# Seven stage boundaries of a two-block transformer kernel, done by token parts, with the double norm's down projection ended tile by tile

## The reference, cut to what matters

```python
def first_block(x, ...):          # two layers
    for i in range(2):
        mix = sconv_ssd_mixer(...) if i % 2 == 0 else fox_mixer(...)
        x = layer_norm(ALPHA * x + mix, ln_mix_g[i], ln_mix_b[i])
        x = layer_norm(ALPHA * x + conv_ffn(x, ...), ln_ffn_g[i], ln_ffn_b[i])
    return x

def second_block(x, c, ...):      # two layers, mod = silu(c) @ ada_w[i] + ada_b[i]
    for i in range(2):
        h = modulate(rmsnorm(x, norm1_g[i]), sh1, sc1)
        y = gqa_attention(h, ...) if i % 2 == 0 else chunked_gmlp(h, ...)
        x = x + g1 * y
        h = modulate(rmsnorm(x, norm2_g[i]), sh2, sc2)
        x = x + g2 * sq_relu_mlp(h, mlp_w_in[i], mlp_w_out[i])
    return x
```

## Time and profile before

| | |
|---|---|
| median of three runs | 2811.45 us (2811.03 to 2812.35) |
| the profiled execution | 2811.43 us, of which 2809.5 us are the profile's span |
| PE busy | 2783.7 us, 99% of the span |
| DVE, ACT, POOL busy | 1303.3, 1081.2 and 1140.6 us |
| granted clock of PE, mean | 0.998 |

### The profile page before, as it was taken

One profiled execution on the slowest core, in us unless ns is written; L12 is line 12 of the kernel. 1 busy time (PEld: TensorE's weight loads), 2 busy tenths in 40 slices (PEclk: granted clock), 3 DMA queues, 4 the chain that ended last, 5 costly groups with the idle time before them and its releaser, 6 DMA issues.

```text
span 2809.5 us, 37915 instructions
## 1 busy us (share of the span) xinstructions
PE 2783.7 (99%) x13890; PEld 2287.7 (81%) x13890; DVE 1303.3 (46%) x1516; ACT 1081.2 (38%) x1574; POOL 1140.6 (41%) x472
## 2 busy tenths in 40 slices
...
GB/s 160 90 69 74 90 103 267 239 140 88 99 88 95 9 76 232 244 169 102 97 73 45 2 74 106 97 105 98 86 135 94 90 78 103 90 92 96 104 98 75
DMA packets 319812, 299.95 MB, mean 107 GB/s; under 512 B 16268, under 2 KB 251224, under 8 KB 319576
## 3 DMA queue, kind: packets, MB, share of 16 engines
...
...
## 4 chain that ended last, share of the span: by engine, by line
PE 46%; issue 36%; POOL 16%; DVE 1%; ACT 0%; POOLq 0%; DVEq 0%; ACTq 0%
POOL wlo L558 16%; PE ps L2034 8%; PE ps L2035 8%; PE ps L2036 8%; PE ps L1892 6%; PE ps L1894 6%; PE ps L1893 6%; PE ps L2319 1%; PE ps L2255 1%; PE ps L2284 1%; PE ps L2394 1%; PE ps L2065 0%; PE ps L2067 0%; PE ps L2066 0%; PE ps L1897 0%
## 5 line engine op out<-in xcount | busy, mean ns | idle before, releaser
L558 POOL TENSOR_TENSOR wlo<-raw,whi 128x1024 fp32r<-128x1024 f32 x444 | 1115.3, 2515 | 1630.6 <-ACT whi L616 1630.3
L1892 PE MATMUL ps<-xhi,whi 128*128 128x512 f32 x1824 | 718.0, 394 | 0.3
L1894 PE MATMUL ps<-xhi,wlo 128*128 128x512 f32 x1824 | 710.3, 389 | 0.0
L1893 PE MATMUL ps<-xlo,whi 128*128 128x512 f32 x1824 | 709.9, 389 | 0.0
L616 ACT ACTIVATE whi<-raw 128x1024 fp32r<-128x1024 f32 x444 | 466.3, 1052 | 288.9 <-PE ps L2036 167.8
L2034 PE MATMUL ps<-whi,ahi 128*128 128x512 f32 x1184 | 461.4, 390 | 0.7 <-DVE alo L1396 0.7
L2036 PE MATMUL ps<-whi,alo 128*128 128x512 f32 x1184 | 460.7, 389 | 0.0
L2035 PE MATMUL ps<-wlo,ahi 128*128 128x512 f32 x1184 | 460.6, 389 | 0.0
L1892 PEld LDWEIGHTS ps<-xhi,whi 128*128 128x128 f32 x1824 | 342.5, 188 | 73.1 <-issue 3.2
L1894 PEld LDWEIGHTS ps<-xhi,wlo 128*128 128x128 f32 x1824 | 342.3, 188 | 71.7
L1893 PEld LDWEIGHTS ps<-xlo,whi 128*128 128x128 f32 x1824 | 342.6, 188 | 71.0 <-issue 1.4
...
## 6 DMA issues: line engine op xcount, KB each, us to landing
...
```

What stands on the lines that cost most here:

```text
L558: pool.tensor_tensor(wlo[:, j], raw[:, j], whi[:, j].bitcast(F32), ALU.subtract).then_inc(w_lo, 1)
L1892: pe.matmul(out, lh, rh, start=start, stop=False)
L1893: pe.matmul(out, lh, rl, start=False, stop=False)
L1894: return pe.matmul(out, ll, rh, start=False, stop=stop)
```

## The change

All seven boundaries run by parts of the tokens. At the six that are called PARTED a part is two tiles: when tiles 0 and 1 are normalized they are transposed and brought to `xhi` and `xlo` as 128 x 256 blocks, and the next projection's first units (in `pe_f` stages units 0, 1 and then 2, with 256 moving columns) take them while tiles 2 and 3 are still on their way. k = 4 to 7 stay whole, their 16 transposes now stand together, and the transposes of constants are gone. At q = 4 the last four units of dn1 run tile by tile (`pe_t_deep`), the parts are tiles (0, 1), 2 and 3, and qkv's first two units follow by these groups. Number 2 of the weight splits moves in ACT's order at q = 1, 2, 3 behind the first part and std(2), at q = 5 and 7 it stands just ahead of the first part.

```diff
-NRM_ORDER = ((0, 0), (1, 0), (0, 1), (2, 0), (3, 0), (1, 1), (2, 1), (3, 1))
-KEEP_BUSY = (0, 18, 0, 16)
+PARTED = (1, 2, 3, 5, 6, 7)
+PART = (slice(0, 256), slice(256, 512))
+DOUBLE_TILES = ((0, 1), (2,), (3,))
+DOUBLE_PART = (slice(0, 256), slice(256, 384), slice(384, 512))
+DEEP = "dn1"
...
+    def act_xt_part(act, q, scale, bias, h, cols=PART):
+        c = cols[h]
+        for k in range(4):
+            act.wait_ge(xt_tp, XT0[q] + 4 * h + k + 1)
             if k >= 2:
-                act.wait_ge(xt_lo, KD * q + k - 1)
+                act.wait_ge(xt_lo, XT0[q] + 4 * h + k - 1)
+            act.activation(xf[:, k % 2, c], ps[:, k, c], ACT.Identity, scale=scale(k), bias=bias(k)).then_inc(xt_ev, 1)
...
         act_next_whi(act, name, 1)
         act_sqrt_table(act, r)
-        for t in range(NT):
-            act_ln_std(act, r, t)
-            if t == 1:
-                act_next_whi(act, name, 2)
+        act_ln_std(act, r, 0)
+        act_ln_std(act, r, 1)
+        act_xt_part(act, r + 1, scale, bias, 0)
+        act_ln_std(act, r, 2)
+        act_next_whi(act, name, 2)
+        act_ln_std(act, r, 3)
         load_gb(act, gb, g_ap, b_ap)
+        act_xt_part(act, r + 1, scale, bias, 1)
+        act_xt(act, r + 1, scale, bias, 4)
...
+    def dve_xt_part(dve, q, h, cols=PART):
+        c = cols[h]
+        for k in range(4):
+            dve.wait_ge(xt_ev, EV0[q] + 4 * h + k + 1)
+            dve.tensor_copy(xhi[:, k, c], xf[:, k % 2, c]).then_inc(xt_hi, 1)
+            dve.wait_ge(xt_hi, XT0[q] + 4 * h + k + 1)
+            dve.tensor_tensor(xlo[:, k, c], xf[:, k % 2, c], xhi[:, k, c].bitcast(F32), ALU.subtract).then_inc(xt_lo, 1)
...
+        for h in range(2):
+            dve_ln_moments(dve, r, name, h and 3)
+            if not h:
+                dve_ln_moments(dve, r, name, 1)
+            for t in (2 * h, 2 * h + 1):
+                dve_ln_inverse(dve, r, t)
+                norm(t, 0)
+            if not h:
+                dve_ln_moments(dve, r, name, 2)
+            dve_xt_part(dve, r + 1, h)
         for t in range(NT):
-            dve_ln_moments(dve, r, name, t)
-            if t:
-                dve_ln_inverse(dve, r, t - 1)
-                norm(t - 1, 0)
-            if t == 2:
-                norm(0, 1)
-        dve_ln_inverse(dve, r, 3)
-        norm(3, 0)
-        for t in range(1, NT):
             norm(t, 1)
+        dve_xt(dve, r + 1, resid=r, k0=4)
...
         dve.wait_ge(gb_in, 32 * (r + 1))
         for t in range(NT):
+            if t == 3:
+                dve_xt_part(dve, 4, 0, DOUBLE_PART)
             dve_ln_moments(dve, r, name, t)
             if t:
-                affine(t - 1)
-            if t >= 2:
-                inverse(t - 2)
-        affine(3)
-        inverse(2)
+                inverse(t - 1)
+            affine(t)
+        dve_xt_part(dve, 4, 1, DOUBLE_PART)
         inverse(3)
+        dve_xt_part(dve, 4, 2, DOUBLE_PART)
...
-            for k in range(KD):
-                pe.wait_ge(xt_lo, KD * q + k + 1)
+            for h in range(2):
+                for k in range(4):
+                    pe.wait_ge(xt_lo, XT0[q] + 4 * h + k + 1)
+                    for e in range(2):
+                        if not h and k == 0:
+                            pe.wait_ge(w_lo, S + e + 1)
+                            pe.wait_ge(res_add, 8 * q - 3 + e)
+                        product(e, k, PART[h])
+                if h:
+                    for k in range(4, KD):
+                        pe_xt_late(pe, q, k)
+                for k in range(4):
+                    if not h and k == 0:
+                        pe.wait_ge(w_lo, S + 3)
+                        pe.wait_ge(res_add, 8 * q - 1)
+                    if not h and k == 3:
+                        pe_xt_part(pe, q, 1)
+                    product(2, k, PART[h])
+            for k in range(4, KD):
+                pe.wait_ge(xt_lo, XT0[q] + 4 + k + 1)
                 for e in range(3):
...
-            if q and q != 4 and t == 2 and i:
-                pe_xt_tile(pe, q, 0)
-        if q:
-            for t in range(0 if q == 4 else 1, NT):
-                pe_xt_tile(pe, q, t)
-                if t == 1:
-                    pe.wait_ge(res_add, 8 * q - 3)
-                pe_busy(pe, KEEP_BUSY[t])
+            if q in PARTED and (t, i) == ((2, 1) if q < 4 else (3, 0)):
+                pe_xt_part(pe, q, 0)
+
+    def pe_t_deep(pe, name, q):
+        H, S, A = PAIRS[name], U0[name], A0[name]
+        for t in range(NT):
+            for m in range(2 * H - 4, 2 * H):
...
+                if t == NT - 1:
+                    ins.then_inc(unit_done, 1)
+                    if m == 2 * H - 3:
+                        pe_xt_part(pe, q, 0)
```

More of the change, by code:

```diff
@@ L618, in build_in, with a_parts @@
     AHEAD = 3
+    def a_parts(name, m):
+        first = 2 * PAIRS[name] - 3
+        if name == DEEP and first <= m < first + 2:
+            return ahi2[:, m - first], alo2[:, m - first]
+        return ahi[:, m % 2], alo[:, m % 2]
     def bank_f(j):
@@ L1407, in dve_jit @@
         after_h0()
-        run(dve, H - 2, lambda e, j: step(H + 2, 2, e, j))
+        if name != DEEP:
+            run(dve, H - 2, lambda e, j: step(H + 2, 2, e, j))
+        else:
+            run(dve, H - 5, lambda e, j: step(H + 2, 2, e, j))
+            for m in range(2 * H - 3, 2 * H):
+                hi, lo = a_parts(name, m)
+                dve.wait_ge(a_hi, A + m + 1)
+                dve.tensor_tensor(lo, src[:, 2 * (m - H):2 * (m - H) + 2], hi.bitcast(F32), ALU.subtract).then_inc(a_lo, 1)
     def wait_tile(eng, r, name, t):
@@ L1653, in dve_rms_tail, with tile @@
         dve.tensor_scalar(mv[:, :, 1], sumsq[:, :, 0], 1.0 / D, EPS, ALU.mult, ALU.add).then_inc(half_sq, 1)
-        for t in range(NT):
+        def tile(t):
             wait_tile(dve, 4 + s, name, t)
             dve_gated_tile(dve, s, 1, t)
-            if t:
-                inverse(t - 1)
-                norm(t - 1, 0)
-            if t == 2:
-                norm(0, 1)
-        inverse(3)
-        norm(3, 0)
-        for t in range(1, NT):
+        tile(0)
+        tile(1)
+        for t in range(2):
+            inverse(t)
+            norm(t, 0)
+        tile(2)
+        dve_xt_part(dve, 5 + s, 0)
+        tile(3)
+        for t in range(2, 4):
+            inverse(t)
+            norm(t, 0)
+        dve_xt_part(dve, 5 + s, 1)
+        for t in range(NT):
             norm(t, 1)
+        dve_xt(dve, 5 + s, k0=4)
     def dve_last_tail(dve, s, name):
@@ L1963, in unit @@
             ins.then_inc(unit_done, 1)
-        for s, v in first:
-            pe.wait_ge(s, v)
         if q == 0:
@@ L2019, in pe_f, with pe_t_unit @@
                     unit(i * RING + j, j)
-    def pe_t_unit(pe, start, e, j, bank0, lh, ll, first, blocks=None):
+    def pe_t_unit(pe, start, e, j, bank0, lh, ll, first, blocks=None, tiles=range(NT), done=True, mid=None):
         slot = (start + j) % RING
@@ L2027, in pe_t_unit @@
         for k in range(2):
+            if mid and k:
+                mid()
             if blocks is not None:
                 pe.wait_ge(xt_lo, blocks + k + 1)
-            for t in range(NT):
+            for t in tiles:
                 out = ps[:, bank0 + t]
@@ L2092, in pe_t_jit @@
             unit(h * H, 0, 0, True)
-            if h:
+            if h and name == DEEP:
+                run(pe, H - 5, lambda e, j: unit(H + 1, e, j, False))
+                pe_t_deep(pe, name, q)
+            elif h:
                 run(pe, H - 3, lambda e, j: unit(H + 1, e, j, False))
```

231 lines of the change are left out of this document (145 added, 86 removed).

## The result

The changed kernel takes 2818.77 us (median of 10 runs, 2817.13 to 2820.53), the kernel before 2811.44 us (10 runs, 2810.41 to 2812.35): 1.0025 times as long, 95% interval 1.0017 to 1.0034. So it is slower, by 7.3 us. Its profiled execution has a span of 2815.8 us, 6.3 us more than that of before; the rest of the 7.3 is told of further down. Its times also scatter more, over 3.4 us against 1.9.

A forecast was written before the change was run, and what follows sets the result against it. PE, busy 99% of the span, was taken as the bound. Terms +5.1 (q=1,2,3), +1.3 (q=5,7), -1.3 (q=6), -5.4 (q=4) and +2.45 (clock) gave +2.1 on 2811.43: 2813.5 us, range 2799 to 2819.

The forecast's parts named there:

- (a) to (f): At q = 1, 2, 3: PE's successive waits through a LayerNorm boundary, the last 2.35 us for block 7, summing to 5.75.
- the first wait: At q = 5 and 7: POOL's split holds the first cast by 1.8 us, PE waits 2.2 before its first product.
- the hold: POOL's weight split and DVE exclude each other, so a DVE cast or subtract beside a split ends about 2 us later.
- the price of q = 1: Waits worked out with q = 1's clock and applied to q = 1, 2, 3 alike: +1.7 us each.
- +1.7 each, +5.1 for three: At q = 1, 2, 3: waits of 5.75 us plus 0.47 for half blocks, less 4.55 saved, at each boundary.
- The wait of 5.0 us at q = 4: PE waits 5.0 us for unit 2's late weight split; the clock then falls to half, costing 2.45 us.
- The rival that the clock falls at other places: Clock also falls in waits at q = 1, 2, 3, 5, 7: +12.3 us, 2825.8; chance 0.15 with dearer 256-column matmuls.
- The holds don't fall on the critical blocks: At q = 1 to 5 and 7 DVE comes before POOL's split, blocks finish in time: -13.5, 2800.1 us; chance 0.20.
- The slower rival: Clock falls at five more boundaries, each costing 2.45 us more: 2825.8 us; chance 0.15 with dearer 256-column matmuls.
- waits of 0.1: At q = 1, 2, 3 from k = 4: DVE takes 2.2 us a block, PE 2.04, giving waits of 0.2, 0.1, 0.1.

The follow-up runs named there:

- Run 3: Changed kernel with part 0 of q = 5 and 7 written by ACT into PSUM and read there by DVE: 2817.43 us.
- run 1: Changed kernel with `wf_lo` made directly behind block 7's `xlo`, ahead of the last three residual operations of q = 2: 2813.27 us.
- run 6: Changed kernel with the residual's four shifts at q = 1, 2, 3 adding only one column of 1024: 2805.99 us.
- run 7: Changed kernel with 34 transposes of constants on PE ahead of its wait for `wf_lo` at q = 2: 2818.08 us.
- run 4: Changed kernel with ACT's split of unit 2 at q = 4 moved just ahead of `xf` block 4: 2814.58 us.
- run 2: Changed kernel with all eight residual operations at q = 1, 2, 3 behind block 7: 2825.78 us.
- run 5: Changed kernel with block 7's cast and subtract ahead of one residual shift, shift(1), at q = 1, 2, 3: 2818.92 us.
- run 8: Kernel before the change without its 34 transposes of constants at each of the seven boundaries: 2826.44 us against 2811.28.
- run 10: Changed kernel with q = 1, 2, 3 as before, the PSUM edit at q = 5 and 7 and q = 4's earlier split: 2801.75 us.
- run 9: Changed kernel with earlier `wf_lo`, block 7 ahead of shift(1), part 0 through PSUM at q = 5 and 7, and q = 4's earlier split: 2803.64 us.

## Why the prediction was right or wrong

**Right: five boundaries and their mechanism.** The waits (a) to (f) at q = 1 and 3 are in the trace in that order, 0.55, 0.34, 0.44, 0.80, short ones, and 1.90 (as the profile counts idle time; from pace to pace the last is 2.06), against forecasts of 0.6, 0.7, 0.6, 1.0, 0.5 and 2.35. The steps came out at 1.6 and 1.9 for a forecast 1.7. The prediction's own list adds up to 5.65 and not 5.75, which changes nothing here. At q = 5 and 7 the first wait is 2.0 for 2.2, at q = 6 the step is -1.4 for -1.3. 256-column matmuls start every 0.12 us, as taken. Run 3 shows the hold to be what it was called, by its operand.

**The time: inside the range by luck.** 2818.77 lies 0.23 us below the range's upper end of 2819, and four of the ten executions lie above it. The forecast of 2813.5 stood for a change that can't be told from none; the measured +7.3 can. Of the 5.3 us between forecast and median, q = 2 has 4.8, the other six boundaries together -0.8, the stretch before the first of them 0.3, and 1.0 is the median above the profiled execution.

**Wrong: one term, q = 2.** The prediction gave all three LayerNorm boundaries the price of q = 1. Of the residual's end it said that nobody waits for it. At q = 2 one reader stands behind it: `wf_lo`, which PE needs right after unit 3, 24 matmuls later. And the chain there begins otherwise. The change also moved the load of `wf_raw` behind the last `xf` (785.60; it was 769.12), which the prediction doesn't name. ACT waited 1.8 us for it, and POOL's split of unit 3 started at 789.20, behind the start of block 7's subtract (788.91), so block 7 wasn't held at all. That the late load set this order is argued; no run puts the load back. The holds fell on the three last residual operations and on `wf_lo`: 4.4 us of wait and 2.5 us of clock in place of the 2.35 us for block 7. The step was +6.5 for a forecast +1.7, and run 1 took 6.8 us away with one moved instruction. So the step that failed is the term "+1.7 each, +5.1 for three": at q = 2 it priced at nothing what stands behind the residual.

**Right in kind, off in size: the clock.** The wait of 5.0 us at q = 4 was 4.75 and did cost the clock, but 1.7 us rather than 2.45, as it fell only at the wait's end; the other waits there came within 0.4 us of their forecast. The step is -3.9 for -2.95. Where in the wait the clock falls differs from profile to profile: in runs 3 and 6 it fell 1.2 and 1.7 us before the end, and the step there is -2.7 and -3.0.

The rival that the clock falls at other places had a point between 1.9 and 2.7 us of wait. There is no such point. Of the profiles with a wait of 1.9 to 2.0 us at the same place, the clock fell in some and not in others:

| wait | fell | not | cost of a fall by the step |
|---|---|---|---|
| block 7 at q = 3, 1.9 us | runs 1, 7 | changed kernel, runs 3, 4 | 1.6 us |
| attention, 1.94 us | runs 2 to 8 and 10 | both kernels, runs 1, 9 | 0.7 to 1.5 us |
| first cast at q = 7, 2.0 us | runs 2, 5 | changed kernel, runs 1, 4, 6, 7 | nothing (0.84 in both, 0.83 without; the wait of 1.1 us behind it is gone in both) |
| block 7 at q = 1, 1.9 us | none | changed kernel, runs 1, 3, 4, 7 | |
| first cast at q = 5, 2.0 us | none | changed kernel, runs 1, 2, 4 to 7 | |

Such falls are the likely reason for the changed kernel's scatter over 3.4 us, and for its median 1 us above the profiled execution. For the other executions there is no trace, but the mean granted clock of each is on record and goes with its time: four at 0.998 took 2817.1 to 2817.7 us (the profiled one is of these), four at 0.997 took 2818.7 to 2819.7, two at 0.996 took 2820.2 and 2820.5. The changed kernel has four such waits at its boundaries, the kernel before none there, and both have the one in the attention. At which wait an execution lost its clock isn't shown.

**The rivals.** "The holds don't fall on the critical blocks" was right for block 7 at q = 2, and they fell on something worse. The slower rival was in part real. What the prediction didn't see is that DVE's backlog stands behind the waits for block 7, for `gt` and for `wf_lo` (run 6 is without all three): part 0 and part 1 cost it 2.8 us each for what four blocks of 512 do in 4.3, and the first conv behind the residual moved from 417.00 to 419.71. The prediction had the pace (2.2 us a block against 2.04) and read it as waits of 0.1; runs 2, 5 and 6 show it as the term that decides where each hold is paid. At q = 1 and 3, while it stands, moving one operation ahead of another only changed the name of the wait; at q = 2 moving `wf_lo` paid, since PE waited for nothing else behind it.
